# Feed-forward adaLN column sums: VectorE transposes, row sums and one constant matmul in place of one-column matmuls

## The chip, the cores and the metric

The kernel runs on one core of one Trainium2 chip. The metric is the device time of one execution in microseconds (us). TensorE (PE in the profile) does matmuls into PSUM, VectorE (DVE), ScalarE (ACT) and GpSimd (POOL) do the elementwise work, and SyncE (SP) issues most of the DMAs. Each engine runs its own instructions in the order in which the program gives them, and waits for the others on semaphores.

## The reference, cut to what matters

Two layers of a small transformer over 256 tokens of width 1024. Each layer has three sublayers: a SwiGLU feed-forward, a token mixer (windowed attention, RG-LRU and gated linear attention in parallel), and a second feed-forward. Each sublayer is modulated by adaLN: nine vectors of 1024 numbers that come from the conditioning vector `c`.

```python
cond = silu(c)                                  # 1 x 1024
for l in range(2):
    mod = cond @ w_ada[l] + b_ada[l]            # w_ada[l] is 1024 x 9216
    (sh1, sc1, g1, sh2, sc2, g2, sh3, sc3, g3) = split(mod, 9)
    h = rms_norm(x, norm_g[l, 0]) * (1 + sc1) + sh1
    x = x + 0.5 * g1 * swiglu(h, w_ff_in[l, 0], w_ff_out[l, 0])
    h = rms_norm(x, norm_g[l, 1]) * (1 + sc2) + sh2
    x = x + g2 * token_mix(h, ...)
    h = rms_norm(x, norm_g[l, 2]) * (1 + sc3) + sh3
    x = x + 0.5 * g3 * swiglu(h, w_ff_in[l, 1], w_ff_out[l, 1])
```

The change is about `cond @ w_ada[l]`, a product of one row with a matrix of 1024 x 9216, all in float32.

## The kernel before, in words

**Main stream.** All large weights pass through as slabs of 128 x 2048 float32 (1 MB). SP loads a slab into one of four `raw` buffers; ScalarE rounds it to `w_hi` (`hi`, L852), VectorE forms the rest `w_lo` (`lo`, L1259), and TensorE multiplies with three products per tile, h_hi and h_lo with w_hi, and h_hi with w_lo (`slab_tile`, L458). A slab is 48 matmuls of 256 columns.

**A feed-forward.** `ff` runs over 11 column groups j. On TensorE an iteration j is: the gate slab of j+1, then the down slab of j (`out_block`), then the up slab of j+1 (in the last but one iteration the up slab comes before the down slab). On VectorE an iteration is: `lo` of the gate slab of j+1, the product with the SiLU (L1334), `lo` of the down slab, the rest of the hidden values (L1338), `lo` of the up slab of j+1, and then the adaLN work. After the last iteration VectorE adds the four banks to the residual stream (`residual`, L1303), ScalarE squares it, TensorE sums the squares over partitions with a matrix of ones (L538), ScalarE forms the reciprocal root (L859, L861), and VectorE and ScalarE make the next h (L1282, L879, L1287). The first product after this that starts with the pieces as they come is L483 (a feed-forward) or L590 (the mixer).

**adaLN.** The 9216 columns of a layer are 18 blocks of 512; a block is two halves of 512 rows of w_ada. For each half VectorE does four steps on 128 x 512 (`weigh`, L1190 and L1196): it multiplies a chunk of 128 rows by cond (a number per partition) and adds it to `ada_acc`. What is left is the sum over the 128 partitions. TensorE does it (`ada`, L494): four matmuls per block, each with 128 columns of `ada_acc` as the stationary operand and one column of ones as the moving one, which leave four columns of 128 numbers in PSUM. VectorE copies them to `mod` (L1205). Of the 36 blocks, 4 are done at the start, 12 in the two mixers, and 20 in the four feed-forwards: 6 each in the two of layer 0 and the first of layer 1, 2 in the last. A table (`FF_HALVES = [0, 2, 2] + [1] * 8`) says how many halves iteration j of a feed-forward weighs, so that blocks are complete at j = 1, 2, 4, 6, 8 and 10. TensorE sums a block right after the gate slab in the iteration after it was completed, and the last one behind the whole feed-forward. `norm` on VectorE waits until `ada_saved` has counted the blocks that it needs.

Of the kernel before, what the change touches and what calls it, by code (L numbers as in the profile page):

```python
# [9 lines left out]
BF16 = mybir.dt.bfloat16  # L10
# [87 lines left out]
def build(nc, x, c, w_ada, b_ada, norm_g, w_ff_in, w_ff_out, w_in, qk_norm_g, attn_sinks, rel_bias,  # L98
# [3 lines left out]
    with ctx:  # L102
        def sb(name, shape, dt=F32):
            return ctx.enter_context(nc.sbuf_tensor(name, [P] + shape, dt))

        def sem(name):
# [57 lines left out]

        ada_acc = scratch[:, 2048:3072].rearrange("p (u n) -> p u n", u=2)

        bias = sb("bias", [HEADS, 192])
        ident, ones, halves = sb("ident", [P]), sb("ones", [P]), sb("halves", [P])
        dup = sb("dup", [2, 2, CH])
        zw = sb("zw", [2 * T], BF16)  # L170
        eps, tiny = sb("eps", [1]), sb("tiny", [1])
# [26 lines left out]
         sq_ready, ss_done, rstd_ready, hf_ready, hhi_ready, h_ready, silu_ready, hid_made, hid_hi_ready, hid_ready,  # L198
         consts_ready, c_loaded, small_loaded, x_loaded, c_turned, turned, x_turned, par_ready, lam_ready, lam_exp,
         cond_ready, rel_saved, rel_stored, bias_loaded, rgw_loaded, rg_done, wg_loaded, alpha_done, kraw_ready, glr_saved,  # L200
# [8 lines left out]
             "sq_ready ss_done rstd_ready hf_ready hhi_ready h_ready silu_ready hid_made hid_hi_ready hid_ready "  # L209
             "consts_ready c_loaded small_loaded x_loaded c_turned turned x_turned par_ready lam_ready lam_exp "  # L210
             "cond_ready rel_saved rel_stored bias_loaded rgw_loaded rg_done wg_loaded alpha_done kraw_ready glr_saved "
# [54 lines left out]
        def ff_closed(l, f, j):  # L266

            first, blocks = ff_ada(l, f)
            return [first + m for m in blocks_closed(FF_HALVES, j) if m < blocks]

        def pair_halves(l, n):
# [175 lines left out]
        def _(pe):  # L447
# [21 lines left out]
            def zero(bank):  # L469
                mm(ps[:, bank, :], zw[:, 0:P], zw[:, :], start=True, stop=False, skip_group_check=True)  # L470

# [15 lines left out]
            def ada(b):  # L487
# [8 lines left out]
                last.then_inc(ada_done, 1)  # L496


            pe.wait_ge(consts_ready, 3)
# [27 lines left out]
            for l in range(DEPTH):  # L527
# [13 lines left out]
                def ff(f, q):  # L541
# [18 lines left out]
                    for j in range(NF):  # L560
                        n = NF * (2 * l + f) + j
                        if j + 1 < NF:
                            pe.wait_ge(silu_ready, n + 1)
                            product(gate_in[j + 1], 4, (h_hi, h_lo))
                        if j > 0:
                            for b in ff_closed(l, f, j - 1):
                                ada(b)
                        if j + 2 == NF:
                            pe.wait_ge(hid_made, n + 1)
                            product(up_in[j + 1], 5, (h_hi, h_lo))  # L570
                        out_block(down[j], j, n + 1, final=j + 1 == NF)
                        if j + 2 < NF:
                            pe.wait_ge(hid_made, n + 1)
                            product(up_in[j + 1], 5, (h_hi, h_lo))
                    for b in ff_closed(l, f, NF - 1):
                        ada(b)

# [582 lines left out]
        def _(dve):  # L1160
# [18 lines left out]

            def weigh(a):  # L1180

                b, q = a // 2, a % 2
                dve.wait_ge(ada_loaded[ada_slot(a)], 32 * (ada_uses(a) + 1))
                if q == 0 and b >= 2:
                    dve.wait_ge(ada_done, b - 1)
                acc, w = ada_acc[:, b % 2, :], ada_raw(a)
                for cc in range(4):
                    by = cond[:, 4 * q + cc:4 * q + cc + 1]
                    if q == 0 and cc == 0:
                        ins = ts(acc, w[:, cc, :], by, None, ALU.mult)  # L1190
                    else:
                        if cc == 0:
                            dve.wait_ge(ada_weighed, a)
                        else:
                            steps.wait()
                        ins = stt(acc, w[:, cc, :], by, acc, ALU.mult, ALU.add)  # L1196
                    if cc < 3:
                        steps.did(ins)
                ins.then_inc(ada_weighed, 1)

            def ada(b):
# [14 lines left out]
            def lam_after():  # L1216
# [22 lines left out]
                steps.did(ts(hcs[:, :], lu[:, 5, :], -4.0, None, ALU.mult))  # L1239
                steps.did(ts(hcn[:, :], lu[:, 5, :], 4.0, None, ALU.mult))  # L1240

            lv = [lu[:, n, :].rearrange("p (l c) -> p l c", l=DEPTH) for n in range(6)]
# [7 lines left out]
            for l in range(DEPTH):  # L1250
# [56 lines left out]
                def ff(e, q):  # L1307
# [5 lines left out]
                    for j in range(NF):  # L1313
# [28 lines left out]
                        if j + 2 == NF:  # L1342
                            lo(down[j])
                        if j > 0:
                            for b in ff_closed(l, e, j - 1):
                                ada(b)
                        for a in ff_halves(l, e, j):
                            weigh(a)
                    gate_column(2 if e == 0 else 8, 6 if e == 0 else 18)
                    for b in range(3):  # L1350
                        residual(b, bank_done, 6 * l + 3 * e + b + 1)
                    residual(3, slab_done, down[NF - 1] + 1)
                    for b in ff_closed(l, e, NF - 1):
                        ada(b)

# [285 lines left out]
```

## Time and profile before

| | |
|---|---|
| median of 3 runs | 1666.35 us (1666.13 to 1666.66) |
| profiled execution | 1667.58 us, of which the profile's span is 1665.8 us |
| TensorE matmul busy | 1578.6 us (95%) |
| TensorE weight load busy | 1531.5 us (92%) |
| VectorE busy | 1086.1 us (65%) |
| ScalarE busy | 810.6 us (49%) |
| DMA | 333.51 MB, mean 200 GB/s |
| granted TensorE clock, mean | 0.982 of full |

Busy times are of instructions that overlap in part, so a busy engine is not at its peak. The chain of work that ended last is followed back from the last instruction, at each step to what released it. One matmul instruction of plain float32 shows as two entries in the trace (two passes); one of the rounded float32 operands as one.

### The profile page before, as it was taken

What the parts mean: (1) busy time and instruction counts of PE and PEld (TensorE: products, weight loads), DVE (VectorE), ACT (ScalarE), POOL (GpSimd) and SP (SyncE); (2) the same over time, 40 slices, a digit from 0 to 9 for tenths busy, and PEclk for the clock granted to TensorE, in tenths of its full rate; (3) what the DMA queues carried; (4) which work ended last, traced back from release to release, by engine and by line L of the source; (5) the groups of instructions that cost most, each with busy time, mean ns of one, the idle gap of its engine ahead of it and who ended that gap; (6) DMA issues with size and microseconds to landing.
All of it is one profiled execution on the core that took longest, in us unless ns stands there. A gap on an engine that the chain in (4) does not pass through costs nothing.

```text
span 1665.8 us, 29385 instructions
## 1 busy us (share of the span) xinstructions
PE 1578.6 (95%) x12723; PEld 1531.5 (92%) x12729; DVE 1086.1 (65%) x1410; ACT 810.6 (49%) x946; POOL 23.3 (1%) x27
## 2 busy tenths in 40 slices
PE   4999999998999998999989999899999999989998
PEld 3999998898998998999989999898899999989998
DVE  6685665787546884665666666569864578657354
ACT  3443345888454444433453333478865444343342
POOL 0000000000100000000000000000001000000000
PEclk8999999999999999999999999999999999999999
DMA  9889654544446874876748767444444588476551
GB/s 327 293 247 262 230 153 142 148 151 127 129 151 228 300 256 159 277 250 225 240 165 280 249 207 229 120 147 133 133 152 128 179 293 299 141 254 201 178 173 55
DMA packets 283743, 333.51 MB, mean 200 GB/s; under 512 B 13084, under 2 KB 234944, under 8 KB 283616
## 3 DMA queue, kind: packets, MB, share of 16 engines
q1 hardware_dynamic: 276816, 327.65, 59.8%
q10 hardware_dynamic: 6800, 4.00, 1.0%
q8 instruction: 100, 1.64, 0.4%
q14 instruction: 27, 0.22, 0.0%
HBM read 330.23 MB, written 1.38 MB: 199 GB/s over the span
## 4 chain that ended last, share of the span: by engine, by line
PE 79%; ACT 9%; DVE 8%; issue 3%; SPq 1%; DMA 0%; ACTq 0%; DVEq 0%
PE ps L458 66%; PE ps L752 3%; PE ps L483 2%; ACT w_hi L852 2%; DVE scratch L1196 2%; PE ps L494 1%; DVE w_lo L1259 1%; DVE scratch L1434 1%; ACT pr L956 1%; ACT pr L954 1%; PE ps L590 1%; PE ps L595 1%; ACT L954 1%; PE ps L717 1%; PE ps L713 1%
## 5 line engine op out<-in xcount | busy, mean ns | idle before, releaser
L458 PE MATMUL ps<-h_hi,w_hi 128*128 128x256 f32 x2464 | 704.5, 286 | 6.6 <-ACT scratch L1049 5.0
L458 PE MATMUL ps<-h_lo,w_hi 128*128 128x256 f32 x2464 | 697.2, 283 | 0.0
L458 PE MATMUL ps<-h_hi,w_lo 128*128 128x256 f32 x2464 | 697.1, 283 | 0.0
L1259 DVE TENSOR_TENSOR w_lo<-raw,w_hi 128x2048 fp32r<-128x2048 f32 x238 | 544.0, 2286 | 154.1 <-ACT w_hi L852 153.6
L852 ACT ACTIVATE w_hi<-raw 128x2048 fp32r<-128x2048 f32 x238 | 453.4, 1909 | 246.8 <-PE ps L458 231.1
L458 PEld LDWEIGHTS ps<-h_hi,w_hi 128*128 128x128 f32 x2464 | 472.7, 192 | 16.1 <-issue 8.5
L458 PEld LDWEIGHTS ps<-h_lo,w_hi 128*128 128x128 f32 x2464 | 472.8, 192 | 2.0 <-issue 1.9
L458 PEld LDWEIGHTS ps<-h_hi,w_lo 128*128 128x128 f32 x2464 | 472.8, 192 | 0.0
L458 PE MATMUL ps<-y_hi,w_hi 128*128 128x256 f32 x704 | 203.0, 288 | 6.9 <-DVE eyr L1518 6.9
L458 PE MATMUL ps<-y_lo,w_hi 128*128 128x256 f32 x704 | 200.5, 285 | 0.0
L458 PE MATMUL ps<-y_hi,w_lo 128*128 128x256 f32 x704 | 200.3, 285 | 0.0
L1196 DVE SCALAR_TENSOR_TENSOR scratch<-eyr,cond,scratch 128x512 f32<-128x512 f32 x252 | 189.3, 751 | 9.1 <-DMA eyr<-in_w_ada_dram 0.3
L1334 DVE TENSOR_TENSOR t512b<-t512a,ps 128x512 f32<-128x512 f32 x44 | 30.3, 688 | 197.0 <-issue 116.6
L458 PEld LDWEIGHTS ps<-y_hi,w_hi 128*128 128x128 f32 x704 | 136.3, 194 | 7.3 <-DVE eyr L1518 7.3
L458 PEld LDWEIGHTS ps<-y_lo,w_hi 128*128 128x128 f32 x704 | 136.5, 194 | 0.0
L458 PEld LDWEIGHTS ps<-y_hi,w_lo 128*128 128x128 f32 x704 | 136.3, 194 | 0.0
L458 PE MATMUL ps<-hid_hi,w_hi 128*128 128x256 f32 x384 | 109.0, 284 | 0.0
L458 PE MATMUL ps<-hid_lo,w_hi 128*128 128x256 f32 x384 | 108.7, 283 | 0.0
L458 PE MATMUL ps<-hid_hi,w_lo 128*128 128x256 f32 x384 | 108.7, 283 | 0.0
L897 ACT ACTIVATE t512a<-ps 128x512 f32<-128x512 f32 x44 | 26.3, 597 | 115.3 <-PE ps L458 100.9
L458 PEld LDWEIGHTS ps<-hid_lo,w_hi 128*128 128x128 f32 x384 | 73.7, 192 | 0.0
L458 PEld LDWEIGHTS ps<-hid_hi,w_hi 128*128 128x128 f32 x384 | 73.7, 192 | 0.0
(247 smaller groups left out, 1635.2 us busy)
## 6 DMA issues: line engine op xcount, KB each, us to landing
raw<-in_w_ff_in_dram SPq DMA_DIRECT2D x176, 512.0 KB, 4.8
eyr<-in_w_ada_dram SPq DMA_DIRECT2D x144, 512.0 KB, 6.6
raw<-in_w_in_dram SPq DMA_DIRECT2D x100, 512.0 KB, 4.7
raw<-in_w_ff_out_dram SPq DMA_DIRECT2D x88, 512.0 KB, 4.7
raw<-in_w_gate_dram SPq DMA_DIRECT2D x48, 512.0 KB, 4.6
raw<-in_w_branch_dram SPq DMA_DIRECT2D x48, 512.0 KB, 4.5
raw<-in_w_out_dram SPq DMA_DIRECT2D x16, 512.0 KB, 4.9
rgw<-in_rg_w_dram ACTq DMA_DIRECT2D x16, 128.0 KB, 2.5
```

The lines of the kernel that those rows point to most:

```text
L458: last = mm(outs, a, b[:, cc, :], start=not rows and cc == 0 and q == 0, stop=cc == n - 1 and q == 2, skip_group_check=True)
L483: last = mm(ps[:, bank, t * T:(t + 1) * T], a, b[:, cc, :], start=False, stop=cc == C - 1 and q == 2, skip_group_check=True)
L494: last = mm(ps[:, 6 + b % 2, t:t + 1], ada_acc[:, b % 2, t * P:(t + 1) * P], ones[:, 0:1], start=True, stop=True)
L590: mm(ps[:, 4, 0:T], wkv[a][:, cc, 0:P], (h_hi, h_lo)[b][:, cc, :], start=cc == 0 and q == 0, stop=cc == C - 1 and q == 2, skip_group_check ...
L595: last = mm(ps[:, 5, m * P:(m + 1) * P], (h_hi, h_lo)[b][:, cc, m * P:(m + 1) * P], wkv[a][:, cc, P:2 * P], start=cc == 0 and q == 0, stop ...
L752: last = mm(ps[:, 1, m * T:(m + 1) * T], a, b, start=cc == 0 and q == 0, stop=cc == C - 1 and q == 2)
L852: f(w_hi[:, p % SPLIT, :], raw[:, p % RAW, :], ACT.Copy).then_inc(hi_ready, 1)
L897: f(t512a[:, :], ps[:, 4, :], ACT.Silu).then_inc(silu_ready, 1)
L954: f(pr[:, hh, 0:P], sc[:, hh, 0:P], ACT.Exp, bias=nmx[:, 0, hh:hh + 1], accum_out=sm[:, 0, hh:hh + 1])
L1196: ins = stt(acc, w[:, cc, :], by, acc, ALU.mult, ALU.add)
L1259: tt(w_lo[:, p % SPLIT, :], raw[:, p % RAW, :], w_hi[:, p % SPLIT, :].bitcast(F32), ALU.subtract).then_inc(lo_ready, 1)
L1334: tt(t512b[:, :], t512a[:, :], ps[:, 5, :], ALU.mult).then_inc(hid_made, 1)
```

## The change

In the four feed-forwards the sum over partitions is done in another way. When VectorE has completed a block it transposes `ada_acc` (128 x 512) in squares of 32 x 32 and sums each row of 32, which leaves 128 x 16 numbers per block in `ada_part`: partition 32q + r holds, for each group of 32 columns, the sum of column r over the 32 partitions of quarter q. What is left is a sum over the four quarters. TensorE does it for a whole group of blocks with one matmul whose stationary operand is the constant `fold` (128 x 128, one where two indices agree modulo 32): the first four blocks (two in the last feed-forward) at j = 8, the other two behind the feed-forward. VectorE copies the result with four copies of 32 partitions each at j = 9 and behind the residual. `weigh` no longer waits for a matmul per block. The start and the mixers keep the one-column matmuls. The constant `fold` is made once at the start on VectorE (one reduction and four copies). Beside this, the zero operand `zw` is half as wide and is read twice through a broadcast by the matmuls that clear a bank (`zero`).

```diff
+        ada_turned = scratch[:, 3072:3584]
+        ada_part = scratch[:, 3584:3680].rearrange("p (b n) -> p b n", b=6)
+        quarter = scratch[:, 1536:1568]
+        fold = sb("fold", [P])
...
-        zw = sb("zw", [2 * T], BF16)
+        zw = sb("zw", [T], BF16)
...
+        def ff_groups(l, f):
+            first, blocks = ff_ada(l, f)
+            return [(first, min(blocks, 4))] + ([(first + 4, blocks - 4)] if blocks > 4 else [])
...
             def zero(bank):
-                mm(ps[:, bank, :], zw[:, 0:P], zw[:, :], start=True, stop=False, skip_group_check=True)
+                mm(ps[:, bank, :], zw[:, 0:P], zw[:, :].unsqueeze(1).broadcast_to((P, 2, T)), start=True, stop=False,
+                   skip_group_check=True)
...
+            def ada_group(l, f, g):
+                first, blocks = ff_groups(l, f)[g]
+                s = first - ff_ada(l, f)[0]
+                pe.wait_ge(fold_ready, 4)
+                pe.wait_ge(ada_folded, folded_before(first + blocks))
+                pe.wait_ge(ada_saved, first)
+                mm(ps[:, 7, 0:16 * blocks], fold[:, :], ada_part[:, s:s + blocks, :].rearrange("p b n -> p (b n)"),
+                   start=True, stop=True).then_inc(ada_done, blocks)
...
                             product(gate_in[j + 1], 4, (h_hi, h_lo))
-                        if j > 0:
-                            for b in ff_closed(l, f, j - 1):
-                                ada(b)
+                        if j == 8:
+                            ada_group(l, f, 0)
...
-                    for b in ff_closed(l, f, NF - 1):
-                        ada(b)
+                    if len(ff_groups(l, f)) > 1:
+                        ada_group(l, f, 1)
...
-            def weigh(a):
+            def weigh(a, stage=None):
...
                 if q == 0 and b >= 2:
-                    dve.wait_ge(ada_done, b - 1)
+                    dve.wait_ge(ada_done, b - 1 if stage is None else stage)
...
+            def fold_block(a, first):
+                b = a // 2
+                dve.wait_ge(ada_weighed, a + 1)
+                steps.did(nc.vector.transpose(ada_turned, ada_acc[:, b % 2, :]))
+                if b == first:
+                    dve.wait_ge(ada_done, first)
+                steps.wait()
+                nc.vector.tensor_reduce(ada_part[:, b - first, :], ada_turned.rearrange("p (n k) -> p n k", k=32), AX.X,
+                                        ALU.add).then_inc(ada_folded, 1)
+
+            def ada_columns(l, f, g):
+                first, blocks = ff_groups(l, f)[g]
+                dve.wait_ge(ada_done, first + blocks)
+                columns = mod[:, :, :].rearrange("p l n -> p (l n)")
+                for q in range(4):
+                    rows = slice(32 * q, 32 * q + 32)
+                    last = cp(columns[rows, 4 * first:4 * first + 4 * blocks],
+                              ps[rows, 7, 0:16 * blocks].rearrange("p (n q) -> p n q", q=4)[:, :, q])
+                last.then_inc(ada_saved, blocks)
...
+            steps.did(nc.vector.tensor_reduce(quarter, ident[:, :].rearrange("p (b r) -> p r b", r=32), AX.X, ALU.add))
+            steps.wait()
+            for q in range(4):
+                cp(fold[:, 32 * q:32 * q + 32], quarter).then_inc(fold_ready, 1)
...
-                        if j > 0:
-                            for b in ff_closed(l, e, j - 1):
-                                ada(b)
+                        if j == 9:
+                            ada_columns(l, e, 0)
                         for a in ff_halves(l, e, j):
-                            weigh(a)
+                            weigh(a, ff_ada(l, e)[0])
+                            if a % 2:
+                                fold_block(a, ff_ada(l, e)[0])
```

How the instructions stand on TensorE, in the first feed-forward, around the sum of one block (before, j = 3; h are the operands of a gate slab, y those of the down slab):

```order
L458 MATMUL ps<-h_hi,w_hi 128x256
L458 MATMUL ps<-h_lo,w_hi 128x256
L458 MATMUL ps<-h_hi,w_lo 128x256
L494 MATMUL ps<-ones,scratch 128x1 [waits ada_saved,ada_weighed]
L494 MATMUL ps<-ones,scratch 128x1 x3
L458 MATMUL ps<-y_hi,w_hi 128x256 [waits hid_ready,lo_ready]
L458 MATMUL ps<-y_lo,w_hi 128x256
```

And in the changed kernel at j = 8, the first place of the feed-forward where anything stands between a gate slab and a down slab (L471 is what was L458):

```order
L471 MATMUL ps<-h_hi,w_hi 128x256
L471 MATMUL ps<-h_lo,w_hi 128x256
L471 MATMUL ps<-h_hi,w_lo 128x256
L520 MATMUL ps<-scratch,fold 128x64 [waits ada_folded,ada_saved,fold_ready]
L471 MATMUL ps<-hid_hi,w_hi 128x256 [waits hid_ready,lo_ready]
L471 MATMUL ps<-hid_lo,w_hi 128x256
```

Six such places of four matmuls become two of one in this feed-forward.

On VectorE, first feed-forward, iteration j = 2, where two halves are weighed and the work on `lam` (L1219 and on, at the start of iteration 3) comes behind; before:

```order
L1259 TENSOR_TENSOR w_lo<-raw,w_hi 128x2048 [waits hi_ready]
L1205 COPY mod<-ps 128x4 [waits ada_done]
L1190 TENSOR_SCALAR scratch<-eyr,cond 128x512 [waits ada_done,ada_loaded2]
L1196 SCALAR_TENSOR_TENSOR scratch<-eyr,cond,scratch 128x512 [waits dve_steps] x3
L1196 SCALAR_TENSOR_TENSOR scratch<-eyr,cond,scratch 128x512 [waits ada_weighed,ada_loaded3]
L1196 SCALAR_TENSOR_TENSOR scratch<-eyr,cond,scratch 128x512 [waits dve_steps] x3
L1219 TENSOR_SCALAR scratch<-scratch 128x16 [waits lam_exp]
```

And the end of a block's work in the changed kernel, one iteration earlier (the same rows stand at j = 2):

```order
L1219 SCALAR_TENSOR_TENSOR scratch<-eyr,cond,scratch 128x512 [waits dve_steps] x3
L1228 STREAM_TRANSPOSE scratch<-scratch 128x512 [waits ada_weighed]
L1232 TENSOR_REDUCE scratch<-scratch 128x16 [waits dve_steps,ada_done]
L1309 TENSOR_TENSOR w_lo<-raw,w_hi 128x2048 [waits hi_ready]
```

The copy with its wait for TensorE is gone from the iteration, and a transpose and a row sum stand between the weighing and the next `lo`.

## Rows read from the trace of the kernel before

**Rows 1.** The page: busy time by engine, and the chain by engine.
```profile
PE 1578.6 (95%) x12723; PEld 1531.5 (92%) x12729; DVE 1086.1 (65%) x1410; ACT 810.6 (49%) x946; POOL 23.3 (1%) x27
...
PE 79%; ACT 9%; DVE 8%; issue 3%; SPq 1%; DMA 0%; ACTq 0%; DVEq 0%
```

**Rows 2.** Windows: two feed-forwards; stretch, its length, busy times, clock, DMA share.
```profile
52.00:243.00 191.00, 189.37 (x1583) 189.20 (x1581) 126.48 (x142) 77.17 (x60) 0.00 (x0) 1.00 0.75 235
659.00:849.00 190.00, 190.00 (x1590) 190.00 (x1588) 121.00 (x116) 74.18 (x57) 0.00 (x0) 1.00 0.68 233
```

**Rows 3.** TensorE's waits in the first feed-forward: total, times, longest.
```profile
PE ps L458 <- DVE w_lo L1259: 1.6, 1, 1.6
```

**Rows 4.** The chain, first feed-forward and behind it: start, length, what.
```profile
52.51 46.08 PE ps L458 x384
98.59 0.79 PE ps L494 x8
...
112.63 5.98 PE ps L458 x48
...
119.39 34.66 PE ps L458 x288
...
243.11 0.79 PE ps L494 x8
243.90 3.58 PE ps L538 x16
```

**Rows 5.** Groups by shape: the one-column matmuls.
```profile
L494 PE MATMUL ps<-ones,scratch 128*128 128x1 f32 x288 | 36.0, 246 | 9.1 <-DVE scratch L1196 9.1
```

**Rows 6.** Timeline of VectorE: start, length, instruction, idle time before it.
```profile
96.34 2.29 DVE L1259 TENSOR_TENSOR w_lo<-raw,w_hi 128x2048 fp32r<-128x2048 f32 x1
99.42 0.16 DVE L1205 COPY mod<-ps 128x4 f32<-128x4 f32 x1 [0.80 <-PE ps L494]
...
110.19 2.28 DVE L1259 TENSOR_TENSOR w_lo<-raw,w_hi 128x2048 fp32r<-128x2048 f32 x1
...
238.90 0.88 DVE L1303 SCALAR_TENSOR_TENSOR xT<-ps,gcol,xT 128x256 f32<-128x256 f32 x2 [1.83 <-PE ps L458]
240.27 0.88 DVE L1303 SCALAR_TENSOR_TENSOR xT<-ps,gcol,xT 128x256 f32<-128x256 f32 x2 [0.49 <-PE ps L458]
...
718.11 0.69 DVE L1334 TENSOR_TENSOR t512b<-t512a,ps 128x512 f32<-128x512 f32 x1 [3.32 <-issue]
...
736.27 0.69 DVE L1334 TENSOR_TENSOR t512b<-t512a,ps 128x512 f32<-128x512 f32 x1 [6.54 <-issue]
```

**Rows 7.** Groups by shape on VectorE: busy, mean ns of one.
```profile
L1190 DVE TENSOR_SCALAR scratch<-eyr,cond 128x512 f32<-128x512 f32 x36 | 17.4, 483 | 6.9 <-DMA eyr<-in_w_ada_dram 6.9
...
L1205 DVE COPY mod<-ps 128x4 f32<-128x4 f32 x36 | 5.7, 159 | 19.4 <-PE ps L494 19.4
...
L1465 DVE TENSOR_REDUCE mx<-scratch 128x4 f32<-128x512 f32 x8 | 5.4, 678 | 0.0
...
L1608 DVE COPY hf<-ps 128x512 f32<-128x512 f32 x2 | 1.4, 692 | 1.4 <-PE ps L810 1.4
```

**Rows 8.** Timeline of ScalarE behind the first feed-forward.
```profile
247.50 0.47 ACT L859 ACTIVATE rstd<-ps,eps 128x256 f32<-128x256 f32 x1 [1.31 <-PE ps L538]
```

**Rows 9.** The chain behind layer 0's second feed-forward and into layer 1.
```profile
848.32 0.89 DVE xT L1303 x2
...
849.77 1.90 ACT w_hi L852
...
858.16 7.39 PE ps L483 x48
```

**Rows 10.** The chain: the same first product, last feed-forward.
```profile
1463.04 8.57 PE ps L483 x48
```

**Rows 11.** Windows around the first products of Rows 9 and 10.
```profile
857.00:862.00 5.00, 3.84 (x20) 3.87 (x21) 4.68 (x12) 3.37 (x8) 0.00 (x0) 0.66 0.90 338
...
1461.00:1469.00 8.00, 5.96 (x28) 5.99 (x29) 7.63 (x16) 4.80 (x9) 0.00 (x0) 0.57 0.67 249
```

More of the change, by code:

```diff
@@ L198, in build @@
          sq_ready, ss_done, rstd_ready, hf_ready, hhi_ready, h_ready, silu_ready, hid_made, hid_hi_ready, hid_ready,
-         consts_ready, c_loaded, small_loaded, x_loaded, c_turned, turned, x_turned, par_ready, lam_ready, lam_exp,
+         consts_ready, fold_ready, ada_folded, c_loaded, small_loaded, x_loaded, c_turned, turned, x_turned, par_ready, lam_ready, lam_exp,
          cond_ready, rel_saved, rel_stored, bias_loaded, rgw_loaded, rg_done, wg_loaded, alpha_done, kraw_ready, glr_saved,
@@ L209, in build @@
              "sq_ready ss_done rstd_ready hf_ready hhi_ready h_ready silu_ready hid_made hid_hi_ready hid_ready "
-             "consts_ready c_loaded small_loaded x_loaded c_turned turned x_turned par_ready lam_ready lam_exp "
+             "consts_ready fold_ready ada_folded c_loaded small_loaded x_loaded c_turned turned x_turned par_ready lam_ready lam_exp "
              "cond_ready rel_saved rel_stored bias_loaded rgw_loaded rg_done wg_loaded alpha_done kraw_ready glr_saved "
@@ L269, in ff_closed, with folded_before @@
             return [first + m for m in blocks_closed(FF_HALVES, j) if m < blocks]
+        def ff_groups(l, f):
+            first, blocks = ff_ada(l, f)
+            return [(first, min(blocks, 4))] + ([(first + 4, blocks - 4)] if blocks > 4 else [])
+        def folded_before(b):
+            return sum(max(0, min(b - first, blocks)) for first, blocks in (ff_ada(l, f) for l in range(DEPTH) for f in range(2)))
         def pair_halves(l, n):
@@ L1352, in ff @@
                     residual(3, slab_done, down[NF - 1] + 1)
-                    for b in ff_closed(l, e, NF - 1):
-                        ada(b)
+                    if len(ff_groups(l, e)) > 1:
+                        ada_columns(l, e, 1)
                 ff(0, 0)
```

## The prediction

> **What bounds the kernel now.** I read the page first, for the engine that the chain lies on, then one window per feed-forward, for how full that engine is where the change is made, then the chain piece by piece inside a feed-forward, and last VectorE's timeline, for the room that its new work has. The page has TensorE busy for 95% of the span and puts 79% of the chain on it [rows 1]. In the first feed-forward TensorE is busy for 189.37 of 191 us, in the second for 190.00 of 190, at full granted clock, while VectorE is busy for 126 and 121 us and ScalarE for less than 80 [rows 2]. Its only wait in the first feed-forward is one of 1.6 us for a `lo` [rows 3], and the second shows none. So a feed-forward is a stream of TensorE instructions end to end, and whatever is taken out of the stream shortens the kernel, as long as VectorE, which is two thirds busy, still delivers in time. The reader should see in the chain that the one-column matmuls are pieces of it: 0.79 us for the eight entries of a block, between pieces of products [rows 4].
>
> **The price of a block on TensorE.** A product runs at 46.08 us for 384 matmuls, 0.12 us each [rows 4]. The pieces that follow a block's sum are longer than that: 288 matmuls take 34.66 us, where 288 times 0.12 is 34.56. So the switch back from the one-column matmuls costs another 0.10 us, and a block inside the stream costs 0.79 + 0.10 = 0.89 us. Behind a feed-forward I count only 0.79. That the entries of these matmuls have a mean of 246 ns [rows 5] is a length with overlap; what counts is the 0.79 / 8 = 0.10 us from one to the next.
>
> **What is removed.** Twenty blocks leave this path, and they do not all pay.
> - Inside the stream lie 5 + 5 + 5 + 2 = 17. The first of them (j = 2 of the first feed-forward) stands ahead of TensorE's only wait, for the `lo` at 110.19 us, and shortens nothing by itself; I treat it below. The other 16 give 16 x 0.89 = 14.24 us.
> - Behind the feed-forwards stand three. After the first feed-forward of a layer the chain goes from the block's sum to the sums of squares (243.11, then 243.90, 3.58 us) [rows 4]. ScalarE has been idle for 1.31 us when that sum comes [rows 8], so it follows if TensorE is early, and the squares of the last bank are needed only by the last quarter of the 3.58 us. Two such places give 2 x 0.79 = 1.58 us. After layer 0's second feed-forward the chain goes another way, from the residual over a `w_hi` to the root on ScalarE [rows 9]: that block is hidden, and gives nothing.
>
> Sum removed: 15.82 us.
>
> **What is added on TensorE.** Seven matmuls, in two passes each, with 64 or 32 moving columns. The trace has none of this shape. From below, a pass cannot be shown to be cheaper than the 0.10 us of the one-column pass, since the stationary operand has the same 128 columns; from above, a plain float32 pass of 256 columns takes 3.58 / 16 = 0.22 us [rows 4]. I take 0.10, as 32 to 64 columns are nearer to one than to 256: 0.20 us per group, plus 0.10 for the switch back where it stands in the stream. Four in the stream are 4 x 0.30 = 1.20, two behind feed-forwards 2 x 0.20 = 0.40, and the seventh is hidden as above: 1.60 us. With the upper bound it would be 1.60 + 6 x 0.24 = 3.0. Their waits (`ada_folded`, `ada_saved`) are satisfied long before: block 4 of a feed-forward is complete at j = 6 and the group stands at j = 8; the last one's fold is done ahead of the last down slab's first bank. The halved zero operand moves the same 512 columns, and I price it at nothing; it lies in TensorE's idle stretch ahead of the products.
>
> **What is added on VectorE.** Per block a transpose and a row sum of 128 x 512. The row sum has a row: 678 ns for a reduction of 128 x 512 [rows 7]. The transpose has none. One-source operations of that size bound it at 483 ns below (a multiply by a scalar) and I bound it above by the 2.28 us of an operation on four times the elements [rows 6]; between them I take the 692 ns of a copy of 128 x 512 [rows 7], which is the plainest pass over the same numbers. Instructions of this length start about 0.09 us before their predecessor's record ends, and each of the two waits for the one before costs some 0.04, so a fold takes 0.60 + 0.60 + 0.08 = 1.28 us of VectorE's time. The 20 small copies of 159 ns [rows 7] become 28, and their waits for TensorE (19.4 us over all blocks) mostly go.
>
> Where does 1.28 us fit? In an iteration with one half (j = 3 to 10) VectorE idles 6.54 us before the next product with the SiLU, in one with two halves 3.32 us [rows 6]. Both hold it, and a later `lo` is still ahead of TensorE. Behind the last iteration the fold stands in front of the residual, where VectorE idles 1.83 us until the first bank is done, and 0.49 before the second [rows 6]; 1.28 fits there too, with 0.55 left. The four copies behind the residual delay a `lo` and the modulation by some 0.25 us, in a stretch in which VectorE waits for ScalarE's root. The constant's five small operations lie at the start, where VectorE waits for the first block of w_ada.
>
> One place is full: iteration 2 of the first feed-forward, where the work on `lam` follows the weighing. VectorE goes from 96.34 to 110.19 with one pause, the 0.80 us for TensorE's sum [rows 6]. In the changed kernel this pause and the copy go (0.80 + 0.08 + 0.04 = 0.92 us) and the fold comes: the `lo` at 110.19 is 1.28 - 0.92 = 0.36 us later. TensorE's product, now at 112.63, starts 0.36 us later instead of 0.89 earlier; TensorE waits there 1.6 + 0.89 + 0.36 = 2.9 us. That is + 0.36 us, and the one block gives nothing.
>
> **Sum.** -15.82 + 1.60 + 0.36 = -13.86 us. On the profiled execution, 1667.58 becomes 1653.7, with a span of 1651.9. The median of the runs lies 1.23 us below the profiled execution, so I forecast 1652.5 us, 0.8% faster. A measurement of this kernel can tell about 0.2%, 3.3 us, from no change.
>
> **What a rule of the skill says.** The row gives the sum over rows 678 ns for 128 x 512 [rows 7], and I count it as hidden. The Trainium skill, page "VectorE: DVE Perf Modes", section "Rules for kernel authors", speaks against such an edit: a `tensor_reduce` on the hot path is the slowest VectorE operation and should be restructured, and chained operations should be kept few. By that rule, if VectorE were the path, the 20 folds would add 20 x 1.28 = 26 us and the kernel would be slower, 1678 us; by the rows of this case they lie in idle time, and the sum above holds. The page "Vector Engine (DVE) Microarchitecture Reference", section 3.8, says that the transpose sustains one element per cycle and lane, which no run here shows yet; by it the transpose would cost about as a copy does.
>
> **The rivals.**
> - *The gain is swallowed by a new wait on VectorE* (slower than before). Let a fold cost F. It costs F - 0.92 in the full iteration; F - 3.3 in the seven other two-half iterations and behind three feed-forwards (1.83 + 3 x 0.49 = 3.3 over four banks); and F - 6.5 in the nine others. Against 14.22 us of net gain on TensorE this breaks even at 11 F = 48.1, F = 4.4 us, that is a transpose of 3.7 us, over five times the copy's 0.69. At F = 5 the time would be 1673 us. For it: the operation has no row, and the page quoted above warns of such work. Against: even an operation on four times the elements takes 2.28. Chance 0.04.
> - *The transpose is dear but hidden in most places*: at 2.28 us F is 2.9, the full iteration costs 2.0 instead of 0.36, and the time is 1654.1 us. It is in the range.
> - *TensorE's clock.* The product that starts as the pieces come took 7.39 us in one place and 8.57 in another [rows 9, 10], with a granted clock of 0.66 and 0.57 of full around them [rows 11]: how long the slow level (1.2 GHz) lasts differs from place to place by over a microsecond. The work moves in time, so these may change, six of them behind the first feed-forward; if three change one way it is 3.5 us. The wait of 2.9 us after 110 us might also bring the slow level, where 1.6 us did not (48 matmuls in 5.98 us [rows 4]); that would be up to 3 us. As a case of its own (gain cut to between 4 and 10 us, 1656.5 to 1662): chance 0.07. As a gain beyond 17 us: 0.03.
> - *It does not do what it says*: the stream is not what sets the end, the matmuls leave and TensorE waits instead, for weights (the DMA share is 0.75 and 0.68 [rows 2]) or ScalarE; 1666 us. Against it is that TensorE waits for no slab in either feed-forward. Chance 0.02.
>
> **How the numbers follow.** The forecast's mechanism has 0.84. Its own bounds: below, 1652.5 less 2.5 for the clock, 1650, and half a microsecond for a transpose at its lower bound with no wait grown, 1649.5; above, + 1.4 for dear group matmuls, + 1.6 for a dear transpose, + 1 for the clock, 1656.5. Faster by over 0.2% are the forecast, the clock cases and what of the VectorE case falls short of break-even: 0.94. Within 0.2%: 0.03. Slower: 0.03.
>
> **What would show it.** In the changed profile the chain of a feed-forward should have no pieces of one-column matmuls, one short piece of about 0.2 us at j = 8, and products at 0.12 us throughout; the one-column group falls from 288 entries to 128, and the new matmul shows 14. The transpose should read about 0.69 us and the row sum 0.68. VectorE's busy time should rise by some 28 us, to about 1115, with TensorE's waits unchanged but for the one behind the full iteration, at 2.9 us. The first feed-forward should end 3.6 us earlier, and the second 4.1 more. I would be wrong if TensorE shows waits for a `lo` in other iterations, if a residual starts late behind its bank, if a product behind the long wait runs at half its rate, or if a block's removal gives 0.79 or less instead of 0.89.

## The result and the profile after

The changed kernel takes 1654.14 us (median, 1653.78 to 1654.50) against 1666.51 us of the kernel before beside it: a ratio of 0.9924, 95% interval [0.9907, 0.9941], or 12.4 us less. The two profiled executions have spans of 1665.8 and 1652.6 us, 13.2 us apart. The forecast was 1652.5 us in a range of 1649.5 to 1656.5.

The page of the changed kernel, busy time by engine and the chain by engine, beside [rows 1]:

```profile
PE 1566.0 (95%) x12583; PEld 1518.5 (92%) x12583; DVE 1116.3 (68%) x1463; ACT 810.5 (49%) x946; POOL 23.3 (1%) x27
...
PE 77%; DVE 9%; ACT 9%; issue 3%; SPq 1%; DMA 0%; ACTq 0%; DVEq 0%
```

TensorE is busy for 12.6 us less and as full as before; VectorE has 30.2 us more to do, and its share of the chain rises by one point. The chain of the changed kernel in the first feed-forward (start, length, what) answers to [rows 4]:

```profile
109.24 2.20 DVE w_lo L1309
...
111.58 93.87 PE ps L471 x768
205.45 0.17 PE ps L520 x2
205.62 34.61 PE ps L471 x288
240.23 0.14 PE ps L520 x2
240.38 3.55 PE ps L562 x16
```

The pieces of 0.79 us are gone, and two short pieces stand in their place, 0.17 and 0.14 us. Two things are to be seen here. The 288 products behind the group take 34.61 us, 0.05 over 288 times 0.12, so the switch back costs half of what it did. And 768 products take 93.87 us where 768 times 0.12 is 92.16: something made this stretch 1.7 us longer. TensorE's waits over the whole span (total, times, longest), and windows behind the long one:

```profile
PE ps L471 <- DVE w_lo L1309: 3.0, 1, 3.0
```

```profile
111.00:113.00 2.00, 1.42 (x10) 1.45 (x11) 2.00 (x3) 0.93 (x2) 0.00 (x0) 0.85 0.25 39
113.00:116.00 3.00, 3.00 (x16) 3.00 (x16) 3.00 (x3) 1.50 (x1) 0.00 (x0) 0.53 0.94 351
116.00:120.00 4.00, 4.00 (x36) 4.00 (x35) 3.69 (x5) 0.60 (x1) 0.00 (x0) 1.00 1.03 335
```

The one wait of [rows 3] has grown from 1.6 to 3.0 us, and behind it the granted clock is 0.53 for 3 us, nearly the lower level (1.2 GHz): 16 products in 3 us, against 36 in the next 4 us. What VectorE's new work costs (groups by shape, beside [rows 7]), and where it fits (timeline of the changed kernel):

```profile
L1228 DVE STREAM_TRANSPOSE scratch<-scratch 128x512 f32<-128x512 f32 x20 | 14.2, 711 | 0.7
L1232 DVE TENSOR_REDUCE scratch<-scratch 128x16 f32<-128x512 f32 x20 | 13.7, 686 | 1.0
```

```profile
97.00 0.48 DVE L1213 TENSOR_SCALAR scratch<-eyr,cond 128x512 f32<-128x512 f32 x1
97.51 5.54 DVE L1219 SCALAR_TENSOR_TENSOR scratch<-eyr,cond,scratch 128x512 f32<-128x512 f32 x7
103.09 0.71 DVE L1228 STREAM_TRANSPOSE scratch<-scratch 128x512 f32<-128x512 f32 x1
...
109.15 2.28 DVE L1309 TENSOR_TENSOR w_lo<-raw,w_hi 128x2048 fp32r<-128x2048 f32 x1
...
236.02 0.88 DVE L1353 SCALAR_TENSOR_TENSOR xT<-ps,gcol,xT 128x256 f32<-128x256 f32 x2 [0.36 <-PE ps L471]
...
241.06 0.68 DVE L1242 COPY mod<-ps 32x8 f32<-32x8 f32 x4
```

From the first row to the `lo` at 109.15 VectorE has no pause (the operations on `lam` fill it from 104.44 on), so it sets the time there. Ahead of the residual 0.36 us of idle time are left of the 1.83 in [rows 6].

**Where the 13.2 us lie.** The chain's marks in both profiles cut the span into pieces. The first product starts at 44.61 before and 42.98 after (-1.63; nothing but the making of the constant lies ahead of it, and the eleven kernels below start it anywhere from 43.0 to 44.2, the three built on the kernel before at 43.5 to 43.7). The four feed-forwards, from their first product to the sums of squares or the end, change by -1.89, -5.18, -3.56 and -1.65; the two mixers, with the norm around them, by +0.89 and -0.18, though nothing is changed there: the +0.89 is one slab that took 7.46 us at 533.78 before and 8.39 us at 530.21 after, each behind the same wait of 3.5 us, with a granted clock of 0.79 and 0.65 in the 8 us from 533 and from 530. In the feed-forwards the first product, which runs in part at the lower clock level, moves by itself (7.91 to 8.00, 8.33 to 7.36, 7.39 to 8.69 and 8.57 to 8.52 us). Without it they change by -1.98, -4.21, -4.86 and -1.60, together -12.65 us.

### The profile page after: what moved, and what is told of

The parts are those of the page before. It is cut to its first block, busy times and chain, and to the rows that moved or that the text cites. A ratio compares the mean times of both kernels' runs of the same rounds, so it can differ in the third digit from the quotient of the medians.

```text
span 1652.6 us, 29150 instructions
## 1 busy us (share of the span) xinstructions
PE 1566.0 (95%) x12583; PEld 1518.5 (92%) x12583; DVE 1116.3 (68%) x1463; ACT 810.5 (49%) x946; POOL 23.3 (1%) x27
## 4 chain that ended last, share of the span: by engine, by line
PE 77%; DVE 9%; ACT 9%; issue 3%; SPq 1%; DMA 0%; ACTq 0%; DVEq 0%
PE ps L471 66%; PE ps L775 3%; PE ps L497 2%; ACT w_hi L875 2%; DVE scratch L1219 2%; DVE w_lo L1309 1%; DVE scratch L1485 1%; ACT pr L979 1%; ACT pr L977 1%; PE ps L618 1%; ACT L977 1%; PE ps L508 1%; PE ps L740 1%; PE ps L736 1%; PE ps L803 1%
## 5 line engine op out<-in xcount | busy, mean ns | idle before, releaser
L471 PE MATMUL ps<-h_hi,w_hi 128*128 128x256 f32 x2464 | 706.1, 287 | 6.9 <-ACT scratch L1072 3.9
L471 PE MATMUL ps<-h_lo,w_hi 128*128 128x256 f32 x2464 | 698.9, 284 | 0.0
L471 PE MATMUL ps<-h_hi,w_lo 128*128 128x256 f32 x2464 | 698.9, 284 | 0.0
L471 PEld LDWEIGHTS ps<-h_hi,w_hi 128*128 128x128 f32 x2464 | 474.1, 192 | 15.9 <-issue 9.9
L471 PEld LDWEIGHTS ps<-h_lo,w_hi 128*128 128x128 f32 x2464 | 474.3, 192 | 2.0 <-issue 1.9
L471 PEld LDWEIGHTS ps<-h_hi,w_lo 128*128 128x128 f32 x2464 | 474.1, 192 | 0.0
L471 PE MATMUL ps<-y_hi,w_hi 128*128 128x256 f32 x704 | 202.8, 288 | 6.9 <-DVE eyr L1569 6.9
L471 PE MATMUL ps<-y_hi,w_lo 128*128 128x256 f32 x704 | 201.2, 286 | 0.0
L471 PE MATMUL ps<-y_lo,w_hi 128*128 128x256 f32 x704 | 201.2, 286 | 0.0
L1219 DVE SCALAR_TENSOR_TENSOR scratch<-eyr,cond,scratch 128x512 f32<-128x512 f32 x252 | 189.3, 751 | 8.9
L471 PEld LDWEIGHTS ps<-y_hi,w_hi 128*128 128x128 f32 x704 | 137.2, 195 | 7.3 <-DVE eyr L1569 7.3
L471 PEld LDWEIGHTS ps<-y_lo,w_hi 128*128 128x128 f32 x704 | 137.1, 195 | 0.0
L471 PEld LDWEIGHTS ps<-y_hi,w_lo 128*128 128x128 f32 x704 | 137.0, 195 | 0.0
L471 PE MATMUL ps<-hid_hi,w_hi 128*128 128x256 f32 x384 | 109.1, 284 | 0.0
L471 PE MATMUL ps<-hid_hi,w_lo 128*128 128x256 f32 x384 | 108.8, 283 | 0.0
L471 PE MATMUL ps<-hid_lo,w_hi 128*128 128x256 f32 x384 | 108.8, 283 | 0.0
L471 PEld LDWEIGHTS ps<-hid_hi,w_hi 128*128 128x128 f32 x384 | 73.8, 192 | 0.0
L471 PEld LDWEIGHTS ps<-hid_lo,w_hi 128*128 128x128 f32 x384 | 73.8, 192 | 0.0
```

What stands on the lines that cost most here:

```text
L471: last = mm(outs, a, b[:, cc, :], start=not rows and cc == 0 and q == 0, stop=cc == n - 1 and q == 2, skip_group_check=True)
```

## The experiments

The theory: in a feed-forward TensorE is the path, a block is worth 0.89 us of it, and VectorE's folds are hidden everywhere but in iteration 2 of the first feed-forward, where the grown wait also brings the slow stretch. The rivals: the matmuls are worth less and the rest comes from VectorE's waits; the folds cost something in many places; the slow stretch has nothing to do with the wait.

**lam_later.** The full iteration is relieved: the work on `lam` moves to iteration 5.

```diff
-                            if j == 3:
+                            if j == 5:
                                 lam_after()
```

> The changed kernel with the work on lam moved from iteration 3 to iteration 5 of the first feed-forward, where one half is weighed. Theory: the 3.01 us for which TensorE waits for a lo there, and the slow clock level behind it (granted 0.53 from 113 to 116 us, products at 0.21 us instead of 0.12), both come from that one full VectorE iteration. Then the wait goes (-3.0 us) and the slow stretch with it (-1.5 us): about 1649.6 us against 1654.1. Rival, the slow stretch falls where it will and not because of the wait: only the 3.0 us go, 1651.1 us, and a slow stretch shows elsewhere in the same feed-forward. Second rival, VectorE has no room at iteration 5 either: a wait of the same size there, no gain.

Measured: 1648.82 us, ratio to the kernel before 0.9892 [0.9877, 0.9906]. The wait for a `lo` is gone from TensorE's waits, and the granted clock is 1.00 from 52 us to the end of the first feed-forward. The gain over the changed kernel is 5.3 us (5.1 by the spans), against 4.5 expected and 3.0 of the rival; from the end of the first product to the sums of squares, the stretch that the edit acts on, it is 4.4 us (189.40 to 184.97). In iteration 5 the margin is thin: the chain has a piece of issue of 0.07 us at 143.51, and the 480 products behind it take 57.82 us where 480 times 0.12 is 57.60.

**before_lam_later.** The same edit in the kernel before.

> The kernel before with the same move of lam. Theory: its wait of 1.63 us and 0.2 us of restart go, 1664.6 us, and the difference between the changed kernel and the kernel before, both with lam moved, is then 15.0 us: 17 blocks of 0.89 in the stream, 2 of 0.79 behind a feed-forward, less 1.2 us of new matmuls, give 15.5. Rival, the one-column matmuls are worth less than 0.89 each in the stream: a difference of 13 us or less.

Measured: 1665.82 us beside 1667.51 of the kernel before, ratio 0.9992 [0.9983, 1.0002]: by the median 1.7 us less, as expected, though the interval holds no change. Against lam_later it is nearly a clean pair: the profile lists no wait for a `lo` in a feed-forward of either. The medians differ by 17.0 us and the spans by 16.5, against the 15.0 expected (15.5 by its terms) and the rival's 13 or less. From the end of the first product to the sums of squares (or the end) the four feed-forwards differ by 4.57, 4.20, 4.87 and 1.52 us. The prices as first read, with 0.22 for a group in the stream and 0.14 behind it, give 5 x 0.89 + 0.79 - 0.36 = 4.88, 5 x 0.89 - 0.22 = 4.23, 4.88 and 2 x 0.89 - 0.22 = 1.56. So a block's price holds in the three to 0.04 us, and is 0.3 short in the first, which is the 0.07 + 0.22 us of iteration 5 above: lam_at_4 (below), where the move to iteration 4 takes them away, has 184.69 us there and differs by 4.85. The four add up to 15.2 us; what the spans have beyond it lies in parts that are alike in both kernels, 1.0 us of it in the mixers. The hidden place behind layer 0's second feed-forward is hidden.

**sums_kept.** The new way, and the old matmuls beside it.

```diff
+            def dummy():
+                for t in range(4):
+                    mm(ps[:, 6, 128 + t:129 + t], ident[:, :], ones[:, 0:1], start=True, stop=True)
...
+                        if j > 0:
+                            for b in ff_closed(l, f, j - 1):
+                                dummy()
...
+                    for b in ff_closed(l, f, NF - 1):
+                        dummy()
```

> The changed kernel with the old one-column matmuls put back on TensorE beside the new way, four of them at each of the 20 old places, with a constant as the stationary operand and a result that nobody reads. They wait for nothing. Theory: TensorE's time for them is the whole gain, so it is lost again: 16 x 0.89 in the stream and 2 x 0.79 behind feed-forwards, +15.8 us less what the first of them fills of TensorE's wait, 1669.5 us with the slow stretch after 112 us as it is. Rival, part of the gain came from VectorE no longer waiting for TensorE (19 us of waits in all before): then less than 15 us come back, 1665 us or below.

Measured: 1669.80 us, ratio 1.0017 [1.0008, 1.0027]. All of the gain is lost again, and 2.8 us more (1669.5 were expected: the new matmuls and the slow stretch stay on top). Its chain has the old pieces back, with the old 0.79 us and the old 0.10 us behind:

```profile
118.76 0.79 PE ps L516 x8
119.55 34.66 PE ps L471 x288
```

VectorE waits for none of these matmuls, and yet the whole gain is gone, so its old waits for TensorE, 19 us in all, had been worth nothing that can be measured.

**three_transposes.** Each fold is made dearer.

```diff
+                for _ in range(2):
+                    steps.did(nc.vector.transpose(ada_turned, ada_acc[:, b % 2, :]))
+                    steps.wait()
                 steps.did(nc.vector.transpose(ada_turned, ada_acc[:, b % 2, :]))
```

> The changed kernel with each block transposed three times instead of once, which adds about 1.5 us of VectorE time to each of 20 folds, 30 us in all. Theory: it is hidden in 19 of them and adds 1.5 us at the full iteration, a wait of TensorE of 4.5 us there, 1655.6 us, up to 1 us more if the slow clock level lasts longer. VectorE's busy time rises to 1145 us. Rival, the folds are partly on the path (a product waits for a lo in other iterations, or a residual starts late): 1660 us or more, with 30 us added 1684 at the most.

Measured: 1656.64 us, ratio 0.9940 [0.9923, 0.9957], 2.5 us above the changed kernel with 28 us more of VectorE work (1144.2 us busy). TensorE's wait is 4.4 us, 1.4 longer, and the 768 products behind it take 95.03 us, 1.2 longer, which accounts for the 2.5. One more wait for a `lo` shows in the whole span, 0.2 us at 901.31 in the first feed-forward of layer 1, so the room of a two-half iteration ends near this size. Timeline of VectorE behind the first feed-forward:

```profile
239.39 0.69 DVE L1235 TENSOR_REDUCE scratch<-scratch 128x16 f32<-128x512 f32 x1
...
240.40 3.41 DVE L1356 SCALAR_TENSOR_TENSOR xT<-ps,gcol,xT 128x256 f32<-128x256 f32 x8
243.72 0.68 DVE L1245 COPY mod<-ps 32x8 f32<-32x8 f32 x4
```

The residual now has no idle time between its banks: it starts late and runs at VectorE's own pace, but TensorE's sums of squares still start 0.15 us after its last matmul. The slack of some 3.3 us over four banks is real, and used up here.

**no_fold.** The transpose and the row sum are replaced by a copy of 16 columns (the column sums are left out in the feed-forwards).

```diff
-                steps.did(nc.vector.transpose(ada_turned, ada_acc[:, b % 2, :]))
...
-                steps.wait()
-                nc.vector.tensor_reduce(ada_part[:, b - first, :], ada_turned.rearrange("p (n k) -> p n k", k=32), AX.X,
-                                        ALU.add).then_inc(ada_folded, 1)
+                cp(ada_part[:, b - first, :], ada_acc[:, b % 2, 0:16]).then_inc(ada_folded, 1)
```

> The changed kernel without the transpose and the row sum: a copy of 16 columns stands in their place, so the column sums are left out in the feed-forwards; the constant matmuls and the copies stay. Theory: the 19 hidden folds were worth nothing, the one in the full iteration 1.3 us, and with a wait of 1.7 us instead of 3.0 the clock stays at its full level (-1.5 us): 1651.3 us. Rival, the folds cost something everywhere (say 0.2 us each by later transfers or contention in SBUF): 1648 us or less.

Measured: 1651.55 us, ratio 0.9908 [0.9893, 0.9922], 2.6 us below the changed kernel. The wait is 1.8 us, 1.2 shorter, and the clock stays full (1.00 from 113 to 120 us); the 768 products behind it take 92.38 us, 1.5 less. The one place accounts for the 2.6 us, so 19 of the 20 folds cost nothing that can be measured.

**before_longer_wait.** The kernel before with two transposes in one iteration, behind `weigh`.

```diff
                         for a in ff_halves(l, e, j):
                             weigh(a)
+                        if l == 0 and e == 0 and j == 2:
+                            for _ in range(2):
+                                dve.wait_ge(ada_weighed, 12)
+                                steps.did(nc.vector.transpose(scratch[:, 3072:3584], ada_acc[:, 1, :]))
+                                steps.wait()
```

> The kernel before with two transposes of 128 x 512 added on VectorE, only behind the weighing of iteration 2 of the first feed-forward, with a result that nobody reads. They make the one wait of TensorE 1.5 us longer, 3.1 us instead of 1.6, and change nothing else. Theory: a wait of 3 us brings the slow clock level behind it in this kernel too: 1.5 us for the wait and 1.5 us for the clock, 3 us above the kernel before. Rival, the slow stretch of the changed kernel came from something else in it: 1.5 us above.

Measured: 1670.31 us beside 1667.00, ratio 1.0022 [1.0013, 1.0032]: 3.3 us above, the theory's 3 and not the rival's 1.5. TensorE's wait is 3.2 us, and the slab behind it (chain of this kernel) takes 8.49 us, where [rows 4] has 5.98 behind 1.6 us:

```profile
112.60 8.49 PE ps L458 x48
121.09 0.79 PE ps L494 x8
```

By this profile the clock costs more than the theory had: from the end of the first product to the sums of squares it is 191.38 us before and 195.49 here, 4.1 more, 1.6 of it the wait and 2.5 the slab. Why the medians show only 3.3 is open; the scatter of the other parts is of that size.

**zero_alone.** The kernel before with the halved zero operand only.

> The kernel before with only the halved zero operand, read twice through a broadcast. Theory: the same, 1666.4 us within 0.7, and a matmul of it shows the same length as before. Rival, it had a part in the 1.5 us that the changed kernel is ahead when its first product starts: 1665 us.

Measured: 1667.04 us beside 1667.00, ratio 1.0003 [0.9994, 1.0013]: nothing. One such matmul has a mean of 437 ns against 445.

**mixers_too.** The same treatment for the blocks of the two mixers (the core of the edit; the transposed copy lies at 4352 in `scratch`).

```diff
-                        for b in pair_closed(l, len(PAIRS) - 1):
-                            ada(b)
...
+                        mm(ps[:, 7, 0:96], fold[:, :], scratch[:, 3072:3168], start=True, stop=True).then_inc(ada_done, 6)
...
-                        weigh(a)
+                        weigh(a, ADA_BLOCKS * l + 10)
+                        if a % 2:
+                            fold_block(a, ADA_BLOCKS * l + 10, scratch[:, 4352:4864],
+                                       scratch[:, 3072:3168].rearrange("p (b n) -> p b n", b=6))
```

> The changed kernel with the same treatment of the 12 blocks of the two mixers: transpose and row sum on VectorE, one constant matmul of 96 columns per layer behind the first output slab. Theory: four blocks per layer leave a stretch that TensorE bounds (-0.89 each), one leaves the place behind the first output slab (-0.65), and two folds per layer fall where VectorE is the path, from 598 to 618 us (+1.35 each, less a copy of 0.1): 2 x (-3.6 - 0.65 + 2.5) = -3.5 us, 1650.6 us. Rival, VectorE is near full over the whole stretch, so that most of the six folds per layer add their 1.35: up to 2 x (-4.2 + 8.1), 1662 us.

Measured: 1654.62 us, ratio 0.9924 [0.9910, 0.9939], the same as the changed kernel: a miss by 4 us, between theory and rival. The first output slab starts 3.0 us earlier (615.86 instead of 618.83), so the matmuls are worth something here too; but TensorE has then waited for 4.8 us in one piece, and the slab runs at the lower level. Its chain, and a window around it:

```profile
613.77 0.72 DVE scratch L1227
...
615.86 5.62 PE ps L497 x24
621.48 0.20 PE ps L822 x2
621.68 17.31 PE ps L471 x144
```

```profile
614.00:622.00 8.00, 6.14 (x30) 6.07 (x31) 6.12 (x8) 2.85 (x3) 0.00 (x0) 0.57 0.15 54
```

In the changed kernel the same window has a clock of 1.00 and two waits of 1.0 us at most. What is gained before the slab is given back in it: the chain's piece behind it starts at 621.68 here and at 621.32 in the changed kernel.

**both.** mixers_too with lam moved.

> The changed kernel with lam moved to iteration 5 and the mixers' blocks folded too. Theory: the two edits lie in different stretches and add, 1646 us if each does what is expected of it alone.

Measured: 1650.89 us, ratio 0.9905 [0.9890, 0.9920]: 3.7 us below mixers_too and 2.1 above lam_later. The 1646 us are missed by what the mixers missed.

**lam_at_4** and **four_and_lam.** lam_at_4 is the changed kernel with lam moved to iteration 4 alone. four_and_lam also folds the first four of the six blocks of each mixer and leaves the last two as they were. The edit of four_and_lam, in parts:

```diff
+                    if s == 11:
+                        first = ADA_BLOCKS * l + 10
...
...
+                        mm(ps[:, 7, 0:64], fold[:, :], scratch[:, 3072:3136], start=True, stop=True).then_inc(ada_done, 4)
...
-                            if j == 3:
+                            if j == 4:
                                 lam_after()
...
+                        if a % 2 and a // 2 % ADA_BLOCKS < 14:
+                            fold_block(a, ADA_BLOCKS * l + 10, scratch[:, 4352:4864],
+                                       scratch[:, 3072:3136].rearrange("p (b n) -> p b n", b=4))
```

> The changed kernel with lam moved to iteration 4 instead of 5. Behind iteration 3 no block is folded, so VectorE has 1.4 us more there; TensorE should show no wait at all in the first feed-forward. Theory: as with lam at iteration 5, 1648.8 us, at most 0.2 less. Rival: with another iteration it is late again, a wait of over 1 us and 1651 us.

> The changed kernel with lam moved to iteration 4, and with the first four of the six blocks of each mixer folded too (one constant matmul for the four, behind slab 11 of the gate and branch pairs). The last two blocks keep their one-column matmuls, since their folds would fall where VectorE is the path. Theory: the mixers gain 4 x 0.89 less 0.22 each, no long wait of TensorE arises ahead of the first output slab, and no slow clock stretch there: 6.7 us below the kernel with lam moved alone (1648.8), 1642.1 us. Rival, VectorE has no room for the first two folds of a mixer either, being busy without a gap from 524 to 543 us: 1645 us or more.

Measured: lam_at_4 1648.37 us, ratio 0.9891 [0.9876, 0.9906], with no wait for a `lo`. Its chain has all products between the first slab and the first new matmul as one piece, 149.76 us, which is 1248 times 0.12:

```profile
51.02 149.76 PE ps L471 x1248
200.78 0.17 PE ps L520 x2
```

four_and_lam 1644.35 us, ratio 0.9866 [0.9851, 0.9880], the fastest kernel of the study, 22.6 us below the kernel before and 9.8 below the changed one. It gains 4.0 us over lam_at_4, not 6.7. From the sums of squares to the first output slab the two mixers gain 2.5 and 2.7 us, not 3.3 each, and its chain now goes through VectorE from 544 us on, folds among it, where that of lam_at_4 is TensorE's products. So VectorE is the path in much of the first mixer's second half, which fits the shortfall, though no run separates it:

```profile
547.50 0.72 DVE scratch L1234
...
548.85 2.28 DVE w_lo L1315
...
560.48 0.72 DVE scratch L1234
```

## Why the prediction was right, point by point

- **TensorE is the path in a feed-forward.** Right. sums_kept gives all of it back.
- **0.89 us for a block in the stream, 0.79 behind a feed-forward, nothing behind layer 0's second.** Right. The pair of before_lam_later and lam_later has 4.20 and 4.87 us where the prices give 4.23 and 4.88. The first feed-forward is 0.3 us short in that pair, and 0.03 with lam_at_4 in the place of lam_later (4.85 for 4.88).
- **The added matmuls, 1.60 us.** Mis-sized, by 0.44 us. A pass takes 0.07 to 0.09 us and not 0.10, and the switch back 0.05 and not 0.10: 4 x 0.22 + 2 x 0.14 = 1.16 us.
- **A fold of 1.28 us.** Close: the transpose is 711 ns for a forecast of 692, the row sum 686 for 678. The Trainium skill's page "Vector Engine (DVE) Microarchitecture Reference", section 3.8, has the transpose at one element per cycle and lane. The prediction took from it a cost about like a copy's, and the trace agrees with that: 711 ns for 512 elements a lane stand beside 692 for the copy of [rows 7]. With one size alone, no run here shows the rate itself.
- **The folds are hidden in 19 of 20 places.** Right: no_fold shows it from one side, three_transposes from the other. The residual keeps 0.36 us of idle time where 0.55 was forecast. The rule of the Trainium skill's page "VectorE: DVE Perf Modes", section "Rules for kernel authors", against a row sum on the hot path did not decide in the feed-forwards, where the sum is hidden in 19 of 20 places; in mixers_too and four_and_lam folds do lie on the chain, and their gains fell short. That the row sum is the slowest operation the trace does not bear out: 686 ns, against 751 for a step of the weighing on as many elements.
- **The full iteration, +0.36 us and a wait of 2.9.** The wait is 3.0 us. From the end of the first product to that restart it is 60.12 us before and 60.61 after, +0.49 where +0.36 was forecast.
- **The clock behind that wait.** This was named as a possible case of up to 3 us and left out of the sum. It happened, and cost 93.87 - 92.16 = 1.7 us, of which 0.2 were there before (5.98 for a slab of 5.76). That is the largest error of a term, and it was one of the prediction's own signs of being wrong (a product behind the long wait at half its rate); lam_later takes the wait and the slow stretch away together, and before_longer_wait brings both with no fold in the kernel.
- **The first feed-forward ends 3.6 us earlier, the second 4.1 more.** The prediction's own terms give 3.49 for the first. In the profiles the sums of squares start 3.52 us earlier, but 1.63 of that is the first product's earlier start: without luck it was 1.9. The second, counted behind its first product, is 4.2.

So the sum over the feed-forwards, -13.86, met -12.65 us: +1.5 for the clock, -0.4 for the group matmuls, +0.1 for the full iteration, and nothing unexplained beyond 0.1. Outside of them, the earlier first product (-1.63) and the mixers (+0.89 and -0.18) differ in parts that the change leaves as they were: the mixers by less than the 1.3 us between those of before_lam_later and lam_later, and zero_alone, whose start is that of the kernel before, has its first product at 43.66 and not at 44.61. So the span of 1652.6 us beside a forecast of 1651.9 is closer than the terms deserve: without the early start it would be 1654.2. The medians, 12.4 us apart, lie 1.5 us short of the forecast, which is the size of the clock's term.

## What to carry to other kernels

Price a small matmul by how far it pushes its neighbours apart in the chain, the switch back to the main stream included, and not by its own record. Work moved to a less busy engine is free only where that engine's idle time lies behind the point at which it delivers: look for the fullest iteration, not at the mean share, and move what stands there too (a `lam` two iterations later was worth 5 us on top of 12). When a change removes work from the bounding engine ahead of one of its waits, it makes that wait longer; a longer wait can cost a second time, by the clock (1.7 us behind the 3.0 here).

## What the hardware showed that was not expected

Inside an otherwise full stream one wait of TensorE of 1.6 us (two kernels) and of 1.8 us left the clock at its full level, and one of 2.1 us (sums_kept, 48 products in 7.49 us), 3.0 us (two kernels), 3.2 us (8.49 us) and 4.4 us was followed by a stretch at the lower level. A slab takes 5.76 us in the full stream, and the products behind the wait took 1.7 us more than their number gives behind 2.1 and 3.0 us, 2.7 behind 3.2 and 2.9 behind 4.4, where 0.2 stood behind 1.6 and 1.8. The waits of 2.5 to 5.2 us between the stages are followed by such a stretch as well. These are six lengths in one place of the kernel, and no bound; and a wait's length does not settle it alone. Each mixer has one wait of TensorE of 2.34 us behind a stream of products. In the changed kernel the clock fell behind the first (at 381.12 us) and stayed full behind the second (at 1185.13):

```profile
381.00:383.00 2.00, 1.88 (x17) 1.48 (x17) 1.93 (x4) 0.78 (x1) 0.00 (x0) 0.76 0.00 0
383.00:385.00 2.00, 2.00 (x5) 1.64 (x6) 2.00 (x2) 1.30 (x2) 0.00 (x0) 0.50 0.00 0
1185.00:1187.00 2.00, 1.87 (x18) 1.65 (x19) 1.93 (x4) 0.80 (x1) 0.00 (x0) 1.00 0.03 8
1187.00:1189.00 2.00, 1.50 (x7) 0.97 (x6) 2.00 (x2) 1.29 (x2) 0.00 (x0) 1.00 0.00 0
```

Over the thirteen profiles the clock fell behind 12 of the 26 waits of this kind, and stayed at 1.00 behind 14. What decides between them no run here shows.
